# Expert routing interleaved with the out projection, no fences around the experts, and an early weight chunk for the next mixer

## The reference, cut to what matters

```
# first block, layer 1
h = h + cross_attention(rms_norm(h), rms_norm(mem)) @ ...     # last step: out projection xa_w_o
hn = rms_norm(h, norm_ffn)
logits = hn @ w_router + b_router                  # 8 experts
top 2 of 8; gates = softmax over the two
h = h + sum over the chosen experts: gate * (silu(hn @ w_gate[e]) * (hn @ w_up[e])) @ w_down[e]   # inner width 3584
# second block, layer 0
hn = rms_norm_2(h, ln_mix_pre[0])
proj = hn @ w_in[0]                                # mixer: query, key and value groups of three attentions
```

## Time and profile before

| | us |
|---|---|
| median of 3 runs | 2725.48 |
| lowest, highest | 2721.44, 2726.2 |
| profiled execution, its own time | 2719.68 |
| its span | 2717.7 |
| mean granted TensorE clock | 0.964 of full speed |

### The profile page before, as it was taken

One profiled execution on the slowest core, in us unless ns is written; L12 is line 12 of the kernel. 1 busy time (PEld: TensorE's weight loads), 2 busy tenths in 40 slices (PEclk: granted clock), 3 DMA queues, 4 the chain that ended last, 5 costly groups with the idle time before them and its releaser, 6 DMA issues.

```text
span 2717.7 us, 39286 instructions
## 1 busy us (share of the span) xinstructions
PE 2575.4 (95%) x16057; PEld 2286.9 (84%) x16057; DVE 1920.2 (71%) x2429; ACT 1494.3 (55%) x1822; POOL 183.6 (7%) x201
## 2 busy tenths in 40 slices
PE   6998989999889899999999999999899999898998
PEld 6766989999779888888888888888797899787998
DVE  6885366544766588989898888888774775665773
ACT  3222365434554377777777777777635564435653
POOL 0000012212010100000000000000000121100120
PEclk9998999999989899999999999999998999889999
DMA  7231044554424299999999999999751455351550
GB/s 220 88 103 47 1 156 137 179 187 154 140 63 140 74 345 356 356 356 361 347 364 341 356 358 353 360 353 361 263 179 42 140 186 165 102 185 47 171 186 32
DMA packets 339194, 567.74 MB, mean 209 GB/s; under 512 B 17592, under 2 KB 184869, under 8 KB 338885
## 3 DMA queue, kind: packets, MB, share of 16 engines
q1 hardware_dynamic: 326394, 556.47, 58.7%
q10 hardware_dynamic: 12618, 8.72, 1.1%
HBM read 564.10 MB, written 2.24 MB: 208 GB/s over the span
## 4 chain that ended last, share of the span: by engine, by line
PE 86%; DVE 6%; ACT 5%; issue 2%; ACTq 1%; POOL 0%; PEld 0%; POOLq 0%; DVEq 0%; PEldq 0%
PE bank L206 22%; PE bank L208 22%; PE bank L207 22%; PE bank L2043 4%; ACT chunks_hi L318 2%; DVE chunks_lo L326 2%; PE bank L3153 1%; PE bank L1715 1%; PE bank L1732 1%; PE bank L3182 1%; PE bank L2576 1%; PE bank L2589 1%; PE bank L2590 1%; PE bank L2095 1%; PE bank L2035 1%
## 5 line engine op out<-in xcount | busy, mean ns | idle before, releaser
L3307 DVE TENSOR_TENSOR weight_lo<-ring,weight_hi 128x2048 fp32r<-128x2048 f32 x336 | 767.0, 2290 | 127.5 <-ACT weight_hi L3242 125.9
L3242 ACT ACTIVATE weight_hi<-ring 128x2048 fp32r<-128x2048 f32 x336 | 643.1, 1917 | 224.0 <-PE bank L208 220.1
L326 DVE TENSOR_TENSOR chunks_lo<-ring,chunks_hi 128x2048 fp32r<-128x2048 f32 x175 | 403.2, 2305 | 305.5 <-ACT chunks_hi L318 305.3
L206 PE MATMUL bank<-x_parts,chunks_hi 128*128 128x256 f32 x1568 | 455.3, 290 | 22.3 <-DVE x_parts L409 13.6
L318 ACT ACTIVATE chunks_hi<-ring 128x2048 fp32r<-128x2048 f32 x175 | 333.4, 1906 | 245.9 <-PE bank L208 241.9
L207 PE MATMUL bank<-x_parts,chunks_hi 128*128 128x256 f32 x1568 | 447.8, 286 | 0.0
L208 PE MATMUL bank<-x_parts,chunks_lo 128*128 128x256 f32 x1568 | 447.7, 286 | 0.0
L206 PE MATMUL bank<-weight_hi,xg_parts 128*128 128x512 f32 x896 | 353.8, 395 | 0.8 <-DVE xg_parts L3313 0.8
L208 PE MATMUL bank<-weight_hi,xg_parts 128*128 128x512 f32 x896 | 350.5, 391 | 0.0
L207 PE MATMUL bank<-weight_lo,xg_parts 128*128 128x512 f32 x896 | 350.0, 391 | 0.0
L206 PEld LDWEIGHTS bank<-x_parts,chunks_hi 128*128 128x128 f32 x1568 | 304.6, 194 | 28.3 <-issue 17.6
(11 more groups left out here) (530 smaller groups left out, 4721.2 us busy)
## 6 DMA issues: line engine op xcount, KB each, us to landing
ring<-in_moe_w_gate SPq DMA_DIRECT2D x112, 1024.0 KB, 6.5
ring<-in_moe_w_up SPq DMA_DIRECT2D x112, 1024.0 KB, 6.7
ring<-in_moe_w_down SPq DMA_DIRECT2D x112, 1024.0 KB, 6.7
ring<-in_w_up SPq DMA_DIRECT2D x44, 1024.0 KB, 5.1
ring<-in_w_in SPq DMA_DIRECT2D x24, 1024.0 KB, 5.3
ring<-in_w_down SPq DMA_DIRECT2D x22, 1024.0 KB, 4.9
ring<-in_xa_w_kv SPq DMA_DIRECT2D x16, 1024.0 KB, 5.5
ring<-in_da_w_qkv SPq DMA_DIRECT2D x12, 1024.0 KB, 5.2
```

What stands on the lines that cost most here:

```text
L206: pe.matmul(dst, l[0], r[0], start=first, stop=False, skip_group_check=True)
L326: dve.tensor_tensor(self.lo[:, n % SPLITS], ring[:, c.slot], self.hi[:, n % SPLITS].bitcast(F32), ALU.subtract).then_inc(self.rest.sem, se ...
L3242: act.activation(weight_hi[:, slot(m, odd + next_)], ring[:, m % RING], ACT.Copy)\
L3307: dve.tensor_tensor(weight_lo[:, at_], ring[:, m % RING], weight_hi[:, at_].bitcast(F32), ALU.subtract)\
```

## The change

1. `out_and_carry` is not called for this projection any more; `moe` holds it. After tile n, TensorE makes the block of k = n-2: two transposes of x tile k into banks 4 to 6, and its two router products into bank 7. The small loads are issued by the scalar engine at tile 0, where the table load stands too. The copies of the turned rows stand behind the square of tile 6 (two), behind that of tile 7 (one), and behind the root (one). They are plain fp32 copies, `xt`, which lies in a slot of `weights.lo`.
2. The fences on both sides of the experts go. A semaphore tells the three engines that the flag is there. The scalar engine splits off the first two expert chunks ahead of it.
3. The gather is 16 plain fp32 products with `xt`; the upper half is rounded from the bank, the lower is the bank less the upper.
4. The mixer's first weight chunk is split beside the last expert's down products. The last four additions raise a semaphore that `enter` waits for tile by tile.
5. `enter` has no sum on GpSimd: `hybrid` sums the squares by eight plain fp32 products with ones (`fold`), one after each k of the first tile. The per-token root is no longer made from sums, but from x_root by four records after tile cq1.

The core of the diff; what is left out are names, the crowded branch and the layout of buffers:

```diff
         def enter(gain, first_chunk):
 
+            arrived = h_new.total - 4
             rebase()
+            flow["x_lo"] = x_lo.total
+            rooms = [x_sum, x_sq[:, 0], x_sq[:, 1]]
 
             @block.scalar
             def _(act):
-                weights.upper(act, first_chunk)
                 for n in range(DT):
+                    if n % 2 == 0:
+                        act.wait_ge(h_new.sem, arrived + n // 2 + 1)
                     carry_hi(act, n, gain, False)
-                    carry_square(act, n)
+                    if n >= 3:
+                        act.wait_ge(x_gathered.sem, x_gathered.at(n - 2))
+                    act.activation(rooms[n % 3], h[:, n], ACT.Square).then_inc(x_squared.sem, x_squared.tick())
...
             def _(dve):
-                weights.lower(dve, first_chunk)
                 for n in range(DT):
                     carry_lo(dve, n, gain, False)
...
+        def fold(pe, n, rooms, squared):
+
+            pe.wait_ge(squared[0], squared[1] + n + 1)
+            mm = pe.matmul(bank[7][:, 0:T], ones[:], rooms[n % 3], start=n == 0, stop=n == DT - 1)
+            told = x_summed if n == DT - 1 else x_gathered
+            mm.then_inc(told.sem, told.tick())
...
         def hybrid(l, plan_, squares=None):
...
+                if squares is not None:
+                    b = next_bank(pe)
+                    weights.need(pe, c_)
+                    for k in range(DT):
+                        marks[order[0]] = part3(pe, b, c_, 0, x_parts, ready, [k], k == 0, k == DT - 1)
+                        if k:
+                            fold(pe, k - 1, *squares)
+                    fold(pe, DT - 1, *squares)
...
                         if key == ("cq", 1):
-                            sum_x(pe, rows=True)
+                            pe.wait_ge(x_rooted.sem, x_rooted.at(1))
+                            for t in range(TT):
+                                mm = pe.matmul(bank[7][:, T + 2 * t:T + 2 * t + 2], x_root[0:1, t * P:(t + 1) * P], ones[0:1, 0:2],
+                                               start=True, stop=True)
+                            mm.then_inc(x_summed.sem, x_summed.tick())
...
+        def moe(c0, o_ready, gain):
...
+            def turned_bank(n):
+                return bank[(4, 5, 6, 4)[n]]
...
+                for n in range(DT + 2):
+                    if n < DT:
+                        marks.append(tile3(pe, c0 + n // 2, n % 2 * P, o_parts, o_ready if n == 0 else None))
+                    k = n - 2
+                    if k < 0:
+                        continue
+                    pe.wait_ge(*ready(k))
+                    if k == 0:
+                        pe.wait_ge(consts_in.sem, consts_in.at(64))
+                    for t in range(TT):
+                        if k == 4 and t == 1:
+                            pe.wait_ge(copied.sem, copied.at(1))
+                        mm = pe.transpose(turned_bank(k // 4 * 2 + t)[:, k % 4 * P:(k % 4 + 1) * P], x[:, k, t * P:(t + 1) * P],
+                                          ident[:])
+                    if k % 4 == 3:
+                        mm.then_inc(turned.sem, turned.tick())
+                    for t in range(TT):
+                        pe.matmul(bank[7][:, t * E:(t + 1) * E], x[:, k, t * P:(t + 1) * P], wr[:, k], start=k == 0 and t == 0,
+                                  stop=k == DT - 1, skip_group_check=True)
...
+                for n in range(DT):
+                    act.wait_ge(evicted.sem, first + n + 1)
+                    if n == 0:
+                        for dst, name in ((wr, "router_view"), (row_b[0:1], "moe_b_router"), (slots, "c_slots"),
+                                          (before, "c_before")):
+                            act.dma_start(dst, ins[name]).then_inc(consts_in.sem, consts_in.tick(16))
+                    carry_square(act, n)
+                    if n == 0:
+                        act.preload_act_table_set(LN_EXP)
+                    if n == 1:
+                        weights.upper(act, c0 + SPLITS)
+                    if n == 6:
+                        copy_of(act, 0)
+                        copy_of(act, 1)
+                copy_of(act, 2)
+                root_x(act, full=False, rows=True, preload=False)
+                copy_of(act, 3)
...
-            end_phase()
...
-                for c_ in range(2):
-                    for half in range(2):
-                        for q in range(4):
-                            m = 4 * half + q
-                            for t in range(TT):
-                                mm = pe.matmul(bank[2 * c_ + half][:, q * P:(q + 1) * P], xt_parts[c_][:, t, m * P:(m + 1) * P],
-                                               to_slot[:, t, 0:P], start=t == 0, stop=t == TT - 1)
-                        mm.then_inc(gathered.sem, 1)
+                for half in range(2):
+                    for q in range(4):
+                        m = 4 * half + q
+                        for t in range(TT):
+                            mm = pe.matmul(bank[half][:, q * P:(q + 1) * P], xt[:, t, m * P:(m + 1) * P], to_slot[:, t, 0:P],
+                                           start=t == 0, stop=t == TT - 1)
+                    mm.then_inc(gathered.sem, 1)
...
+                        if m == NC - 4 and last:
+                            upper_ahead(act)
...
-                        dve.tensor_copy(xg_parts[:, 1, 4 * half:4 * half + 4],
-                                        bank[2 + half][:, :].rearrange("p (a b) -> p a b", b=P)).then_inc(tokens_lo.sem, 1)
...
+                        dve.tensor_tensor(xg_parts[:, 1, fs], bank[half][:, :].rearrange("p (a b) -> p a b", b=P),
+                                          xg_parts[:, 0, fs].bitcast(F32), ALU.subtract).then_inc(tokens_lo.sem, 1)
...
+                act.wait_ge(routed.sem, routed.at(1))
+                for m in range(2):
+                    upper(act, 0, m, 0)
+                act.wait_ge(crowd_known.sem, crowd_known.at(1))
...
-            end_phase()
```

More of the change, by code:

```diff
@@ L351, in tile3, with part3 @@
                 weights.need(pe, c)
+            return part3(pe, b, c, a, x, ready)
+        def part3(pe, b, c, a, x, ready=None, ks=range(DT), first=True, last=True):
             w = weights.view(c)
-            for k in range(DT):
+            for k in ks:
                 if ready is not None:
                     pe.wait_ge(*ready(k))
-                mm = three(pe, b[:, 0:T], [v[:, k, a:a + P] for v in w], [x[:, i, k] for i in range(2)], k == 0, k == DT - 1)
-            mm.then_inc(tiles_done.sem, tiles_done.tick())
-            weights.done[c] = tiles_done.total
+                mm = three(pe, b[:, 0:T], [v[:, k, a:a + P] for v in w], [x[:, i, k] for i in range(2)],
+                           first and k == ks[0], last and k == ks[-1])
+            if last:
+                mm.then_inc(tiles_done.sem, tiles_done.tick())
+                weights.done[c] = tiles_done.total
             return tiles_done.total
@@ L1569, in _ @@
                            .then_inc(squared.sem, squared.tick())
+                    if key == ("cq", 1) and squares is not None:
+                        act.wait_ge(x_summed.sem, x_summed.at(2))
+                        act.activation(x_col[:, 0:4], bank[7][:, T:T + 4], ACT.Copy).then_inc(x_rooted.sem, x_rooted.tick())
                     if key in used_up:
@@ L1600, in _ @@
                         r = x_col[:, 2 * t:2 * t + 1]
+                        if n == 0 and squares is not None:
+                            dve.wait_ge(x_rooted.sem, x_rooted.at(2))
                         if n < 2:
@@ L2841, in moe @@
             count, crowd = take(E), take(E)
-            top = take(8, TT)
+            top, row_l = take(8, TT), take(E)
             routing = used[0]
-            x, row_l = x_plain, take(E)
+            x = x_plain
             assert used[0] <= NORM_AT
             consts_in = sig("consts_in")
-            ready = x_ready()
+            turned, copied, routed, chosen, placed = (sig(n) for n in ("turned", "copied", "routed", "chosen", "placed"))
+            crowd_known = sig("moe_crowd")
+            halves = [(t, half) for half in range(2) for t in range(TT)]
```

211 lines of the change are left out of this document (110 added, 101 removed).

## The result

| | before | after |
|---|---|---|
| median of the runs (14 each), us | 2724.08 | 2728.79 |
| lowest, highest | 2720.83, 2727.09 | 2722.69, 2734.23 |
| ratio, 95% interval | | 1.0018, 1.001 to 1.0026 |
| profiled execution, its span | 2717.7 | 2732.3 |
| mean granted clock in it | 0.964 | 0.959 |

The change cost 4.7 us. Forecast was a gain of 7.5, to 2718.0. So the first step is to cut both spans at the same four places of TensorE's timeline: the first product of the out projection, the first expert product, the first product of `leave` behind the last expert, and tile 2 of the next mixer.

What follows compares the result with a forecast made beforehand. TensorE, busy 95% of the span, was taken as the bound, with slack only at the seams around the experts. Terms 2.5 + 3.0 - 1.0 + 3.0 = 7.5 us gained, median 2725.48 to 2718.0, range 2711 to 2726.

Steps and rivals of the forecast that it cites:

- The 991 us of the experts: Experts, 953 to 1944 us: TensorE waited 0.8 us there, once, so moving their start leaves their length alone.
- the seven gathers: Gathers inside the experts: both kinds cost the same at full clock, so nothing, at most +-0.5 us in all.
- Seam 1 as work: Out projection to first expert product: routing interleaved into the projection, fences gone, shorter tail after the gather; 2.5 us gained.
- the wait of 1.4: Out projection, block of k = 4: TensorE waits 1.4 us for the first copy of xt to free bank 4.
- The clock in the gather: First gather: plain fp32 products raise the clock, speeding it and the first expert products; 3.0 us gained.
- The clock at the added wait: Out projection after tile 6: the wait might drop the clock, 2.5 us if it falls; taken as -1.0.
- Rival B: Out projection: interleaved tiny products pull the clock down throughout; 5.5 us slower, 2732; chance 0.07.
- Seam 2: Experts' end into the next mixer: early weight chunk and sums on TensorE start tile 2 earlier; 3.0 us gained, at most 4.2.
- the wait for the root: Next mixer, before tile 2: TensorE waits 1.3 us for the finished root; a clock drop there costs 1.7.
- the early drop: Next mixer's first products: if the clock drops first, last fold and root move by 2.8 or so, leaving 1.2 us gained.
- Which engine is late: Scalar engine: its copy of xt holds up the block of k = 4, its root holds up the mixer's tile 2.
- rival C: Whole kernel: both clock effects come out well, no wait of 1.3 at the root; 10 to 12 us gained, 2714.5; chance 0.20.

Runs made afterwards that it cites:

- g1: Changed kernel with its activation parts and the six weight slots behind them 48 words higher; 2713.37 us against 2722.77 for the kernel before (0.9962).
- i1: Kernel before with upper weight slots 16 words off the held operands, lower ones on their grid; 2749.90 us in one execution, 2722.84 beside it.
- g3: Kernel before with its four lower weight slots 48 words higher; 2729.9 us (ratio 1.0032).
- f3: Kernel before with the change's buffer places, activation parts and six slots 8 words up, token parts and lower slots 0, 1 8 words down; 2733.04 us (1.0038).
- e1b: Kernel before with the change's buffer places, but token parts at 5904, activation parts at 7952, lower slot 3 at 25408; 2736.24 us (1.0048).

## Why the prediction was wrong, step by step

g1 is the change with the layout put right, so its seams can be held against the forecast.

- **"The 991 us of the experts are therefore left alone by anything that only moves their start", and the seven gathers "give nothing, at most +-0.5".** This is the step that failed, by 11.7 us (1001.42 in after, 989.69 in g1). Its reason, that TensorE waits for next to nothing there, was right and is still right in after. It does not follow that the products keep their length. The diff also moved buffers, so that for all gate and up products and half of the down products held and streamed operand no longer leave the same remainder to 64 words, and that took 0.2295 to 0.233 us per gate and up product in place of 0.2275. The prediction had no term for it, and no rival had it either.
- **Seam 1 as work, 2.5 us, and the wait of 1.4.** Right: a block 0.59 for 0.70, the wait 1.34, the row sums 3.2 earlier for 3.0. The four small loads were hidden.
- **The clock in the gather, +3.0.** Right in kind, and somewhat small: the first expert product comes 4.56 us earlier (forecast "5 us or so"), and the warm first chunk takes another 2.2 off the experts (989.69 in g1 for 991.85). Seam 1 gives 6.7 in g1, where 2.5 + 3.0 - 1.0 = 4.5 was forecast.
- **The clock at the added wait, -1.0.** It did not fall (1.00 from 930 to 934.8). Rival B, the clock pulled down over the projection, is shown wrong by the same windows, and no alternation of the clock is seen there, as the rule of the Trainium skill weighed in the prediction (TensorE: Matmul & The Clock Gate, A second HAM failure mode: psum-queue depth-cycling) would have had it.
- **Seam 2, 3.0 us.** 2.7 in after and 3.8 in g1 at tile 2, less 1.5 for the drop behind the wait for the root: 1.2 and 2.3 net. This is the least certain term: the same stretch took 20.83 in the profile of before, but 21.1 to 22.6 in the thirteen experiments that leave its code alone. The wait for the root was 1.39 (forecast 1.3). In after the eight folds ran wholly at full clock, so the early drop that was weighed did not come.
- **Which engine is late.** As forecast at both places, the scalar engine: L2940 at the block of k = 4, L443 at tile 2.

The net of these, 6.7 + 2.3 = 9.0, agrees with the 9.4 us that g1 gained, and lies between the forecast of 7.5 and rival C; with the spread of seam 2, so close an agreement is in part luck. In the changed kernel as it was given, it went under in a stretch that the argument had set aside. Its time came nearest to that of rival B, whose mechanism the windows refute.

## What to carry to other kernels

In a stretch that TensorE bounds, "it waits for nothing" does not mean "nothing can change": compare the distance between the starts of the same product before and after. For products like these, keep the places of a product's held and streamed operands, both parts of split ones too, equal to a remainder of 256 bytes in the partition, and treat every moved buffer in a diff as a step that needs a term. A profile of one execution has some 5 us of clock luck in stretches that nobody touched, so cut both spans at the same instructions before reading a difference.

## What the runs showed of the hardware

- fp32r products of 512 columns go at 0.2275, 0.2293 or 0.233 us, by the distance of their two operands' places (remainder to 256 bytes), with nothing else moved. Distances of 16 words for the upper half and 0 for the lower (i1) cost as much as 48 throughout, though 16 throughout costs a third of it, and though 0 and 48 (g3) or 32 and 0 (f3) cost no more than that third. Why is open.
- Products on the grid that follow products off it are slower at first: nine at 0.2305, then 0.2267 (e1b, slot 2).
- With 16 plain fp32 products of 128 columns TensorE's clock rose inside the first gather (0.68 over 6.1 us); with the same work as fp32r products it did not in 7.9 us. What went on just before was the same in kind, so the form of the product is the likely cause; no run here changes the form alone.
- Behind the wait for the root the clock fell some 1 us after the products had begun again, and stayed at half for 3.2 us.
